# Swapping two declarations: the normalised activations' hi/lo pair and the gains-and-x tensor change places in a partition

## The reference

```python
def first_block(x, ...):                      # depth 1
    h = rms_norm(x, norm_mix)
    aq, ak, av, rq, rk, rv, rg, ga, gr = split(h @ w_in)      # 1024 -> 5888
    att = sliding_window_attention(aq, ak, av, att_sinks)
    ret = head_group_norm(retention_chunkwise(rq, rk, rv), ret_gn_gain) * silu(rg)
    x = x + (sigmoid(ga) * (att @ w_att_o) + sigmoid(gr) * (ret @ w_ret_o)) @ w_out
    h = rms_norm(x, norm_ffn)
    x = x + (silu(h @ w_gate) * (h @ w_up)) @ w_down
    return rms_norm(x, final_norm)

def second_block(x, ...):
    proj = rms_norm_2(x, ln_mix_g) @ w_in
    a = gmlp_spatial_gating(...); b = banded_chunk_attention(...)
    x = x + concatenate([a, b]) @ w_out
    return x + peer_ffn(rms_norm_2(x, ln_ffn_g), w_query, sub_keys, expert_u, expert_v)

def peer_ffn(x, ...):        # 8 heads, 16 experts each, of 16384 experts
    eidx, g = the 16 best of the products of two sub-key scores, and their softmax
    h = gelu(einsum('thkd,td->thk', expert_u[eidx], x))
    return einsum('thk,thkd->td', g * h, expert_v[eidx])
```

## Time and profile before

| | |
|---|---|
| median of three runs | 1181.62 us |
| the profiled execution's own time | 1181.62 us |
| its span, from the first to the last instruction | 1179.9 us |
| outside the span | 1.7 us |
| mean granted TensorE clock | 0.984 of full speed |
| read from the chip's memory | 367.82 MB, 313 GB/s over the span |

### The profile page before, as it was taken

How to read it: one execution, slowest core, us unless ns; L and a number is a source line. 1 busy time by engine, 2 the same in 40 slices (tenths; PEclk the granted TensorE clock), 3 DMA queues, 4 the chain that set the end, 5 groups by cost and what they waited for, 6 DMA issues and landing times.

```text
span 1179.9 us, 13282 instructions
## 1 busy us (share of the span) xinstructions
PE 1051.6 (89%) x3820; PEld 663.2 (56%) x3820; DVE 809.7 (69%) x1695; ACT 613.0 (52%) x1347; POOL 318.7 (27%) x283
## 2 busy tenths in 40 slices
PE   8999999999999999998999898878787776877777
PEld 7788878888888877885545454423232222332232
DVE  5763667765545588868697776776676677667755
ACT  7464554554445467835664555445434544544453
POOL 1000000100000000023355454445545444554451
PEclk9999999999999999998999999999989999999999
DMA  9463337955635654569999999999999999999997
GB/s 322 144 207 114 128 124 247 313 179 180 195 104 169 240 186 173 199 222 401 398 420 421 421 421 421 421 421 422 420 421 422 420 410 424 406 422 422 423 422 300
DMA packets 95761, 369.50 MB, mean 313 GB/s; under 512 B 6544, under 2 KB 30104, under 8 KB 63072
## 3 DMA queue, kind: packets, MB, share of 16 engines
q0 software_dynamic: 38464, 273.46, 56.3%
q1 hardware_dynamic: 57248, 95.45, 24.3%
HBM read 367.82 MB, written 1.06 MB: 313 GB/s over the span
## 4 chain that ended last, share of the span: by engine, by line
PE 51%; DMA 19%; DVE 15%; issue 6%; ACT 4%; POOL 4%; SPq 0%; POOLq 0%; DVEq 0%; ACTq 0%
DMA uv_ring<-in_peer_uv,expert 18%; PE gemm L1682 12%; PE gemm L2092 11%; PE gemm L1684 11%; PE gemm L1683 11%; DVE uv_ring L1570 4%; POOL uv_ring L479 4%; PE trb L1676 2%; DVE w_both L976 1%; PE mmb L1764 1%; DMA x_sb<-in_x 1%; ACT diag L934 1%; DVE hit L1517 1%; DVE hit L1519 1%; DVE picked L1520 1%
## 5 line engine op out<-in xcount | busy, mean ns | idle before, releaser
L2092 PE MATMUL gemm<-uv_ring,diag 128*128 128x512 f32 x1020 | 489.6, 622 | 112.1 <-ACT diag L934 111.7
L479 POOL DMA_INDIRECT uv_ring<-in_peer_uv,expert x256 | 307.4, 1201 | 398.4 <-PE gemm L2092 267.2
L2092 PEld LDWEIGHTS gemm<-uv_ring,diag 128*128 128x128 f32 x1020 | 189.0, 196 | 384.9 <-ACT diag L934 210.5
L1570 DVE CUSTOM_DVE_ANT_0 uv_ring<-uv_ring,gains_xT 128x1024 f32<-128x1024 f32 x256 | 309.2, 1223 | 139.0 <-DMA uv_ring<-in_peer_uv,expert 138.9
L976 DVE TENSOR_TENSOR w_both<-raw,w_both 128x1024 fp32r<-128x1024 f32 (+1 forms) x184 | 193.2, 1062 | 148.2 <-ACT w_both L532 147.7
L532 ACT ACTIVATE w_both<-raw 128x1024 fp32r<-128x1024 f32 (+1 forms) x184 | 168.7, 927 | 178.3 <-PE gemm L1684 176.7
L1683 PE MATMUL gemm<-w_both,hT_hi 128*128 128x512 f32 (+1 forms) x592 | 228.0, 385 | 0.0
L928 ACT ACTIVATE hid_g<-hid,scales 128x1 f32<-128x1 f32 x256 | 74.9, 293 | 281.6 <-DVE hid L1570 279.6
L1682 PE MATMUL gemm<-w_both,hT_hi 128*128 128x512 f32 (+1 forms) x544 | 216.6, 398 | 4.6 <-DVE w_both L976 4.3
L1684 PE MATMUL gemm<-w_both,hT_lo 128*128 128x512 f32 (+1 forms) x544 | 209.4, 385 | 0.0
L1683 PEld LDWEIGHTS gemm<-w_both,hT_hi 128*128 128x128 f32 x592 | 111.9, 189 | 26.5 <-issue 7.0
(11 more groups left out here) (277 smaller groups left out, 903.8 us busy)
## 6 DMA issues: line engine op xcount, KB each, us to landing
raw<-in_w_in SPq DMA_DIRECT2D x30, 1024.0 KB, 5.1
raw<-in_w_gate SPq DMA_DIRECT2D x22, 512.0 KB, 4.0
raw<-in_w_up SPq DMA_DIRECT2D x22, 512.0 KB, 5.0
raw<-in_w_down SPq DMA_DIRECT2D x22, 512.0 KB, 3.3
raw<-in_w_out SPq DMA_DIRECT2D x8, 1024.0 KB, 5.1
uv_ring<-in_peer_uv,expert POOLq DMA_INDIRECT x258, 13.4
raw<-in_w_ret_o SPq DMA_DIRECT2D x4, 1024.0 KB, 5.1
raw<-in_peer_w_query SPq DMA_DIRECT2D x4, 1024.0 KB, 5.1
```

Source lines behind the costliest of these rows:

```text
L479: nc.gpsimd.indirect_dma_start(out=uv_ring[k % RING][:, 0:width], out_offset=None, in_=peer_uv, in_offset=bass.IndirectOffsetOnAxis(ap=exp ...
L1570: V.tensor_tensor_reduce(out=u_row, in0=u_row, in1=xn[:, b, :], scale=1.0, scalar=0.0, op0=ALU.mult, op1=ALU.add, accum_out=hid[par][:, k: ...
L2092: last = nc.tensor.matmul(gemm[2 * b + n][:], diag[k % 4][:], uv_ring[k % RING][:, D + n * CHUNK:D + (n + 1) * CHUNK], start=(begin and k ...
```

## The change

The declaration of `hT` moves behind those of `gains_xT` and of its two views. No instruction, no wait, no offset within the slab and no size changes. Row for row, the instruction lists of PE, DVE, ACT, POOL and SP are the same before and after (2054, 1150, 917, 132 and 74 rows).

```diff
         x_sb = sb("x_sb", [P, TB, D])
-        hT = [sb("hT_hi", [P, KD, S], f32r), sb("hT_lo", [P, KD, S], f32r)]
         gains_xT = sb("gains_xT", [P, G_COLS + TB * D])
         gains = gains_xT[:, 0:G_COLS]
         xn = gains_xT[:, G_COLS:G_COLS + TB * D].rearrange("p (b d) -> p b d", b=TB)
+        hT = [sb("hT_hi", [P, KD, S], f32r), sb("hT_lo", [P, KD, S], f32r)]
```

## The result

The changed kernel is slower. Its median over five runs is 1188.39 us (1187.49 to 1189.77), against 1182.07 us for the kernel before on the same chip (1181.37 to 1182.84). The ratio is 1.0053, with a 95% interval of 1.0039 to 1.0068. The profiled execution took 1187.22 us with a span of 1185.5 us, 5.6 us more than before in both.

The account below looks back on a forecast made before the run. The prediction took PE to bound the kernel up to 540 us and the gathers' transfers after it. Its terms, 0 + 0 + 0, left the profiled 1181.62 us unshifted: 1181.6 us, range 1179.8 to 1184.4 us.

Parts of the forecast that it names:

- What bounds the kernel: Whole kernel: dense products up to 540 us bound by PE, 97% busy; gathers from 600 to 1160 us bound by transfers.
- hT as PE's weights: Matmuls with weights from hT, 1728 in or near the PE-bound part: new address costs 0, bounds 8.6 us slower, 3.5 us faster.
- the comparison of the two places: Before 540 us: 512-column matmuls follow at 226 ns with weights from hT, 227 ns with ffT, so place costs 0.
- So the remainder costs and gives nothing here, to the ns: PE's transposes: weight loads take 140 ns from xn (remainder 0) and from proj (remainder 128), so hT's changed remainder costs nothing.
- The cover of 38 ns: PE's weight loads: a 188 ns load under a 226 ns matmul leaves 38 ns, so slightly longer loads would not show.
- The dots and the DMAs of the moved tensors, 0,: DVE's dots reading xn, median 1224 ns, and transfers into gains_xT or out of xn: unchanged by the move, cost 0.
- TensorE is slowed at its new weights: Rival, before 540 us: each of 1728 matmuls with hT takes 5 ns more, 8.6 us, giving 1190.2 us; chance 3%.

## Why the prediction was wrong

*What bounds the kernel* held. The part before 540 us was PE's, all of the loss fell there, and the gather stage didn't move.

*hT as PE's weights, cost taken 0,* is the step that failed: "I take 0, because the comparison of the two places is the nearest there is." The two places differ by about 100 KB, but `hT`, `ffT` and `w_both` all start 128 past a multiple of 256. Every pair in that trace that is a 512-column product of line 1682 to 1684 had equal remainders. The comparison varied the one thing that doesn't count and held fixed the one that does. In the sum this term was 0; it measured 4.5 ns a matmul and 5.9 us in all. The experiments put the step at 227 ns for equal remainders (at 128, 192, 0 past a multiple of 256) and at 232 to 234 for 32, 64 or 128 ahead.

*"So the remainder costs and gives nothing here, to the ns"* failed in two ways. It looked at the load of the weights, and loads didn't change in the changed kernel either; the matmul did. And it compared transposes, of 128 columns against `ident`, where even different pairs step at 109 ns. A remainder of a single tensor is no property that matters here, as the kernels with everything moved show; the difference between two is.

*The cover of 38 ns* was of no use. It would hide a longer load, and the load was not longer.

*The dots and the DMAs of the moved tensors, 0,* held: 1224 ns, and `gains_xT` moved alone gave 1.0005 (0.9995 to 1.0014).

*The rival "TensorE is slowed at its new weights"* was what happened, at a chance of 3%. Its price was 1728 x 5 ns = 8.6 us, 1190.2 us; measured 1188.39. The 5 ns was near (4.5), but 144 of the 1728 matmuls have 256 columns and lost nothing. The other 1584 x 4.5 ns make 7.1 us, and 5.9 arrived at the first dot. Step against step in the two traces, up to the first dot, the undisturbed steps of 512 columns with `hT` grew by 6.8 us in all, and all other steps together took 0.9 us less. The rival's source for the 5 ns, the query products at 394 ns, was no sign of it: they are at 393 ns in the changed kernel, against 394 in the earlier trace rows. In the gather stage steps of 229 and 232 ns stand in the kernel before too, with equal remainders. That the price came so near was luck.

The prediction let the Trainium skill, page "SBUF — State Buffer", section "SBUF: two separate sides", speak for its 0. That section names where engines and transfers can hinder one another and says nothing of a tensor's place within its partition, so the 0 did not follow from it. What the runs show: moving `hT` by 8 KB and more costs nothing, and 32 bytes against its partner cost 5 ns a matmul. The warning in the same page of the Trainium skill, section "Operand start alignment", that its runs timed nothing, was the one to weigh more.

What stays open: why unequal remainders cost TensorE time, and why 64 behind costs 2 ns where 64 ahead costs 6. No run here separates mechanisms for it. It is also not separated which of the slab's tensors brings the gather its gain. The slots of the ring are the obvious ones, as the gathers write there, but the indices moved along.

## What to carry to other kernels

When a change moves tensors, work out the remainder by 256 of every operand, and compare pairs that are read by one matmul, before and after; a trace where all pairs are alike says nothing on another relation. Two places that cost the same are evidence only if they differ in what may count. Start the big allocation at a multiple of 256 bytes and keep all others in step: here one declaration of 128 bytes ahead of the slab was worth 0.7%.

## What the runs showed of the hardware

- Up to 540 us, 512-column fp32r matmuls follow each other in 227 ns where weights and moving operand have equal remainders by 256, in 232 to 234 ns where the weights are 32, 64 or 128 ahead, in 229 ns where they are 64 behind. The granted clock was 1.00 in that window. With 256 columns nothing is lost (120 ns, down to 116 with 64 ahead). Other differences, and ones that are no multiple of 32 bytes, were not run.
- Gathers of 8 KB rows ran at 420 to 421 GB/s into a slab 128 or 192 bytes past a multiple of 256, and at 424 to 425 into one at a multiple. The mean time of a packet of 8192 bytes between 700 and 1100 us of the packets' own record was 314.9 ns before, 314.5 with everything moved by 64, 311.0 with 128 and 310.6 with the changed order aligned. The Trainium skill, page "DMA: Bandwidth & Descriptors", section "How a descriptor splits into AXI transactions", says that a descriptor that does not start at a multiple of 256 bytes begins at the boundary below and pays for it. The gain of 1.2% in the packets' time agrees in sign. But the page speaks of what is fetched, and here it was the written side that moved, so no run shows that this is the cause.
